# Queries from unnormalised rows, with the norm's factor applied later

## The reference, cut to what matters

```python
x = x + mixed @ w_out[l]
x = x + peer(rmsnorm(x, norm2_g[l]), peer_w_query[l], peer_sub_keys[l], peer_u[l], peer_v[l])
...
q = (xt @ w_query).reshape(T, PEER_HEADS, 2, PEER_DK // 2)
s = jnp.einsum('thpd,phkd->thpk', q, sub_keys)
s_top, i_top = lax.top_k(s, PEER_TOPK)
cand = s_top[:, :, 0, :, None] + s_top[:, :, 1, None, :]
best, pos = lax.top_k(cand, PEER_TOPK)
g = jax.nn.softmax(best, axis=-1)
a = gelu(einsum('thkd,td->thk', u_tab[idx], xt))
out = einsum('thk,thkd->td', g * a, v_tab[idx])
```

## Time and profile before

| what | value |
|---|---|
| median of 3 runs | 1877.42 us (1875.99 to 1878.51) |
| profiled execution | 1873.26 us, span 1871.5 us |
| granted TensorE clock, mean | 0.998 |
| TensorE busy | 1843.8 us, 99% |
| VectorE busy | 1381.0 us, 74% |
| ScalarE busy | 1170.2 us, 63% |
| GpSimd busy | 754.7 us, 40% |

### The profile page before, as it was taken

One profiled execution on the slowest core, in us unless ns is written; L12 is line 12 of the kernel. 1 busy time (PEld: TensorE's weight loads), 2 busy tenths in 40 slices (PEclk: granted clock), 3 DMA queues, 4 the chain that ended last, 5 costly groups with the idle time before them and its releaser, 6 DMA issues.

```text
span 1871.5 us, 38820 instructions
## 1 busy us (share of the span) xinstructions
PE 1843.8 (99%) x11090; PEld 1591.0 (85%) x11090; DVE 1381.0 (74%) x3018; ACT 1170.2 (63%) x2296; POOL 754.7 (40%) x586
## 2 busy tenths in 40 slices
PE   7999999999999999999999999999999999999998
PEld 6889888888888888778888998888888888888886
DVE  6864998888887666776647559987888966666666
ACT  5754666777776555555566446667777765555554
POOL 6551998677770000010063439967777500000000
PEclk9999999999999999999999999999999999999999
DMA  6345555444445575555542545554444455555554
GB/s 217 101 134 160 180 191 191 158 154 146 148 146 180 191 243 206 185 180 186 193 143 76 169 155 188 185 188 162 146 148 145 150 187 196 195 191 191 193 195 150
DMA packets 90500, 320.04 MB, mean 171 GB/s; under 512 B 10304, under 2 KB 11072, under 8 KB 90176
## 3 DMA queue, kind: packets, MB, share of 16 engines
q1 hardware_dynamic: 90432, 319.20, 49.9%
HBM read 318.11 MB, written 1.05 MB: 171 GB/s over the span
## 4 chain that ended last, share of the span: by engine, by line
PE 93%; DVE 3%; ACT 1%; issue 1%; POOL 1%; DMA 0%; SPq 0%; POOLq 0%; DVEq 0%; ACTq 0%
PE ps L919 26%; PE ps L921 13%; PE ps L994 12%; PE ps L996 12%; PE ps L997 12%; PE ps L941 5%; PE ps L892 2%; PE ps L890 2%; PE ps L895 2%; ACT work L1146 1%; PE ps L906 1%; PE ps L605 0%; PE ps L800 0%; PE ps L744 0%; POOL tab_lo L1431 0%
## 5 line engine op out<-in xcount | busy, mean ns | idle before, releaser
L919 PE MATMUL ps<-x_hl,tab_hi 128*128 128x512 f32 x2048 | 725.9, 399 | 0.0
L1492 POOL TENSOR_TENSOR tab_lo<-raw,tab_hi 128x512 fp32r<-128x512 f32 x448 | 575.2, 1298 | 254.6 <-ACT tab_hi L1272 167.0
L921 PE MATMUL ps<-x_hl,tab_lo 128*128 128x256 f32 x2048 | 571.4, 279 | 0.0
L2071 DVE TENSOR_TENSOR tab_lo<-raw,tab_hi 128x512 fp32r<-128x512 f32 x512 | 356.1, 697 | 256.2 <-ACT tab_hi L1384 254.7
L919 PEld LDWEIGHTS ps<-x_hl,tab_hi 128*128 128x128 f32 x2048 | 384.4, 188 | 89.8 <-DVE tab_lo L1965 0.3
L1272 ACT ACTIVATE tab_hi<-raw 128x512 fp32r<-128x512 f32 x504 | 316.0, 630 | 196.5 <-PE ps L921 195.5
L994 PE MATMUL ps<-tab_lo,w_hi 128*128 128x512 f32 x1024 | 399.4, 390 | 0.7 <-DVE w_lo L2111 0.7
L996 PE MATMUL ps<-tab_hi,w_hi 128*128 128x512 f32 x1024 | 398.5, 389 | 0.0
L997 PE MATMUL ps<-tab_hi,w_lo 128*128 128x512 f32 x1024 | 398.4, 389 | 0.0
L921 PEld LDWEIGHTS ps<-x_hl,tab_lo 128*128 128x128 f32 x2048 | 386.0, 188 | 0.0
L1384 ACT ACTIVATE tab_hi<-raw 128x512 fp32r<-128x512 f32 x512 | 320.2, 625 | 92.9 <-PE ps L997 92.2
(11 more groups left out here) (226 smaller groups left out, 2327.5 us busy)
## 6 DMA issues: line engine op xcount, KB each, us to landing
raw<-tab_u SPq DMA_DIRECT2D x256, 512.0 KB, 3.2
raw<-tab_v SPq DMA_DIRECT2D x256, 512.0 KB, 3.2
raw<-w_proj SPq DMA_DIRECT2D x64, 512.0 KB, 3.6
raw<-w_proj SPq DMA_DIRECT2D x16, 384.0 KB, 3.1
work<-cdft SPq DMA_DIRECT2D x8, 256.0 KB, 5.9
work<-sub_keys SPq DMA_DIRECT2D x2, 1024.0 KB, 4.9
work<-pmat SPq DMA_DIRECT2D x4, 304.0 KB, 5.2
x<-x_in SPq DMA_DIRECT2D x2, 512.0 KB, 3.8
```

The costliest lines, as they stand in the source:

```text
L919: mm(ps[:, s, :], hi, x_hl[:, 4 * h + k, :, :].rearrange("p a t -> p (a t)"), start=(h + k == 0), stop=False, skip_group_check=True)
L921: last = mm(ps[:, s, 0:256], lo, x_hi[:, 4 * h + k, :], start=False, stop=(h + k == 4), skip_group_check=True)
L1492: tt(half(tab_lo, s, h), half(raw, s, h), half(tab_hi, s, h).bitcast(F32), ALU.subtract).then_inc(lo_pool.sem, 1)
L2071: v.tensor_tensor(half(tab_lo, s, h), half(raw, s, h), half(tab_hi, s, h).bitcast(F32), ALU.subtract).then_inc(lo_dve.sem, 1)
```

## The change

The rows of x are transposed as they are, without the scaling. Their row pieces (times the gain) go into `x_hi` and `x_lo` and the queries are made from them. TensorE drops the 14 filler matmuls; it transposes channels 0 to 511 (`transpose_rows(0)`, 8 transposes) ahead of query tile 0 and channels 512 to 1023 (`transpose_rows(4)`) behind it. The row pieces are laid so that pieces 0 to 3 fill banks 4 and 5, pieces 4 to 7 banks 6 and 7.

The factor of a token, still the inverse root from GpSimd, is used twice. The exponential of the softmax takes it as its scale, one instruction per block of tokens. For the experts, VectorE multiplies the identity by the factor (`scale_diagonal`), TensorE multiplies ones by that diagonal ahead of query tile 6, which puts the factor of each token in every partition, and ScalarE copies it to SBUF. From the end of query tile 8 on, GpSimd adds the two parts of row piece k and multiplies by the factor (`scale_rows(k)`) as soon as query tile 8+k has used it; ScalarE and VectorE split the result again (`scaled_upper`, `scaled_lower`). TensorE waits for the eighth piece ahead of the experts.

```diff
@@ TensorE
+                def transpose_rows(k0):
+
+                    for b in range(TB):
+                        pe.wait_ge(*at(out_added, l, 12 if k0 else 10 + b))
+                        for k in range(k0, k0 + 4):
+                            last = tr(row_tile(k)[:, b * P:(b + 1) * P], x[:, b, k * P:(k + 1) * P], ident)
+                    last.then_inc(xT_ready.sem, 2)
...
-                keep_clock(14, 1)
-                transpose_x(2, 4)
+                transpose_rows(0)
                 keep_clock(3, 1)
 
                 for n in range(16):
                     part, k = n // 8, n % 8
+                    if n == 1:
+                        transpose_rows(4)
+                    if n == 6:
+                        pe.wait_ge(*at(h_lo, l, 2 * DT))
+                        pe.wait_ge(*at(diag_ready, l, TB))
+                        for b in range(TB):
+                            last = mm(ps[:, 7, b * P:(b + 1) * P], ones, diag[:, b, :], start=True, stop=True)
+                        last.then_inc(scale_ready.sem, 1)
+                    if n == 8:
+                        pe.wait_ge(*at(scale_taken, l, 1))
...
+                pe.wait_ge(*at(scaled_lo, l, DT))
                 u_product(0, True, lo_pool, LO_E)
@@ ScalarE
+                def rows_upper(start, end):
+                    for k in range(start, end):
+                        if k % 4 < 2:
+                            act.wait_ge(*at(xT_ready, l, 6 + 2 * (k // 4)))
+                        else:
+                            act.wait_ge(*at(h_lo, l, DT + k - 1))
+                        fn(x_hi[:, k, :], row_tile(k), ACT.Copy, scale=par("g2", k)).then_inc(h_hi.sem, 1)
...
+                block_squares(0)
+                rows_upper(0, 2)
                 upper(Q0 + 1, 0)
                 upper(Q0 + 1, 1)
-                transposed_upper("g2", 8, 4)
+                rows_upper(2, DT)
+                block_squares(1)
                 for n in range(Q0 + 2, Q0 + 10):
+                    if n == Q0 + 8:
+                        act.wait_ge(*at(scale_ready, l, 1))
+                        fn(token_scale, ps[:, 7, 0:256], ACT.Copy).then_inc(scale_taken.sem, 1)
                     upper(n, 0)
                     upper(n, 1)
...
                 for n in range(Q0 + 10, U0 + 1):
                     upper(n, 0)
                     upper(n, 1)
+                    if n > Q0 + 10:
+                        scaled_upper(n - Q0 - 11)
...
-                fn(best.rearrange("p b h n -> p (b h n)"), best.rearrange("p b h n -> p (b h n)"),
-                   ACT.Exp).then_inc(gate_exp.sem, 1)
+                for b in range(TB):
+                    last = fn(best[:, b, :, :], best[:, b, :, :], ACT.Exp, scale=rinv[:, b:b + 1])
+                last.then_inc(gate_exp.sem, 1)
@@ GpSimd
+                def scale_rows(k):
+
+                    pool.wait_ge(*at(half_used, l, 2 * (Q0 + 8 + k) + 2))
+                    if k >= 2:
+                        pool.wait_ge(*at(scaled_lo, l, k - 1))
+                    tt(scaled[k % 2], x_hi[:, k, :].bitcast(F32), x_lo[:, k, :].bitcast(F32), ALU.add)\
+                        .then_inc(row_sum.sem, 1)
+                    pool.wait_ge(*at(row_sum, l, k + 1))
+                    tt(scaled[k % 2], scaled[k % 2], token_scale, ALU.mult).then_inc(row_scaled.sem, 1)
...
+                pool.wait_ge(*at(scale_taken, l, 1))
+                for k in range(DT - 2):
+                    scale_rows(k)
+                u_lower_half(0, 0, 0)
+                scale_rows(DT - 2)
+                u_lower_half(0, 0, 1)
+                scale_rows(DT - 1)
+                u_lower(0, 1)
@@ VectorE
-                add_group(2, 1, HYENA_BANKS, (1,), (0,))
-                block_mean(0)
-                add_group(2, 1, HYENA_BANKS, (1,), (1,))
-                block_scale(0)
-                block_mean(1)
-                block_scale(1)
-                transposed_lower("g2", 8, 4, 0, 2)
+                add_group(2, 1, HYENA_BANKS, (1,))
+                rows_lower(0, 2)
                 lower(Q0 + 1, 0)
                 lower(Q0 + 1, 1)
-                transposed_lower("g2", 8, 4, 2, DT)
-
+                rows_lower(2, DT)
                 for n in range(Q0 + 2, U0):
                     lower(n, 0)
                     lower(n, 1)
+                    if n == Q0 + 3:
+                        block_mean(0)
+                        block_mean(1)
+                    if n == Q0 + 4:
+                        scale_diagonal(0)
+                        scale_diagonal(1)
+                    if n >= Q0 + 11:
+                        scaled_lower(n - Q0 - 11)
+                scaled_lower(DT - 3)
...
+                scaled_lower(DT - 2)
+                scaled_lower(DT - 1)
```

More of the change, by code:

```diff
@@ L146, in hybrid_encoder, with row_tile @@
         columns = [onehot[:, s, 8 * P:10 * P].bitcast(BF16).rearrange("p (t c) -> p t c", t=4) for s in range(2)]
+        diag = dist_abs[:, 0:TB, :]
+        def row_tile(k):
+            col = (k // 2 % 2) * 256
+            return ps[:, 4 + k % 2 + 2 * (k // 4), col:col + 256]
+        token_scale = sums[:, 0, 0, :]
+        scaled = [sums[:, 1, n, :] for n in range(2)]
         picksf = picks[:, :, :].rearrange("p n t -> p (n t)")
@@ L287, in hybrid_encoder @@
         inv_root = sig("inv_root", 6)
-        xn_done = sig("xn_done", 2 * TB)
+        xn_done = sig("xn_done", TB)
         xT_ready = sig("xT_ready", 8)
@@ L291, in hybrid_encoder @@
         h_lo = sig("h_lo", 16)
+        diag_ready = sig("diag_ready", TB)
+        scale_ready = sig("scale_ready", 1)
+        scale_taken = sig("scale_taken", 1)
+        row_sum = sig("row_sum", DT)
+        row_scaled = sig("row_scaled", DT)
+        scaled_hi = sig("scaled_hi", DT)
+        scaled_lo = sig("scaled_lo", DT)
         fn_m_ready = sig("fn_m_ready", 1)
@@ L1055, in transposed_upper, with scaled_upper @@
                            scale=par(gain, k)).then_inc(h_hi.sem, 1)
+                def rows_upper(start, end):
[5 more added lines that the diff above has]
+                        fn(x_hi[:, k, :], row_tile(k), ACT.Copy, scale=par("g2", k)).then_inc(h_hi.sem, 1)
+                def scaled_upper(k):
+                    act.wait_ge(*at(row_scaled, l, k + 1))
+                    fn(x_hi[:, k, :], scaled[k % 2], ACT.Copy).then_inc(scaled_hi.sem, 1)
                 def spectrum_part(n, bank):
@@ L1241, in _, with block_squares @@
                 upper(Q0, 1)
[L1242 to L1246, removed]
+                def block_squares(b):
+                    for n in range(2 * b, 2 * b + 2):
+                        act.wait_ge(*at(out_added, l, 8 + n + 1))
+                        col = slice((n % 2) * 512, (n % 2 + 1) * 512)
+                        fn(xn[:, n // 2, col], x[:, n // 2, col], ACT.Square, scale=D ** -0.5,
+                           accum_out=ss4[:, n:n + 1]).then_inc(sq_sum.sem, 1)
+                block_squares(0)
+                rows_upper(0, 2)
                 upper(Q0 + 1, 0)
                 upper(Q0 + 1, 1)
-                transposed_upper("g2", 8, 4)
+                rows_upper(2, DT)
+                block_squares(1)
                 for n in range(Q0 + 2, Q0 + 10):
+                    if n == Q0 + 8:
+                        act.wait_ge(*at(scale_ready, l, 1))
+                        fn(token_scale, ps[:, 7, 0:256], ACT.Copy).then_inc(scale_taken.sem, 1)
                     upper(n, 0)
@@ L1258, in _ @@
                     upper(n, 1)
+                    if n > Q0 + 10:
+                        scaled_upper(n - Q0 - 11)
                 upper(U0 + 1, 0)
+                scaled_upper(DT - 2)
                 upper(U0 + 1, 1)
+                scaled_upper(DT - 1)
                 for g in range(4):
@@ L1485, in _, with u_lower_half, u_lower @@
                     inverse_root(5 + b, rinv[:, b:b + 1], ms[:, b:b + 1], 1)
-                def u_lower(i):
-                    for s in range(4):
+                def u_lower_half(i, s, h):
+                    pool.wait_ge(*at(half_used, l, i * 8 + 2 * (U0 + s) + h - 3))
+                    pool.wait_ge(*at(hi_done, l, i * 8 + 2 * (U0 + s) + h + 1))
+                    tt(half(tab_lo, s, h), half(raw, s, h), half(tab_hi, s, h).bitcast(F32),
+                       ALU.subtract).then_inc(lo_pool.sem, 1)
+                def u_lower(i, first=0):
+                    for s in range(first, 4):
                         for h in range(2):
[L1490 to L1493, removed]
+                            u_lower_half(i, s, h)
                 def set_ones(start, end):
@@ L1498, in set_ones @@
                     return nc.gpsimd.memset(area(start + P, end - start - P), 1.0)
+                def scale_rows(k):
[6 more added lines that the diff above has]
+                    tt(scaled[k % 2], scaled[k % 2], token_scale, ALU.mult).then_inc(row_scaled.sem, 1)
                 pool.wait_ge(*at(xT_ready, l, 8))
                 set_ones(UNIT_A, CAND).then_inc(unit_set.sem, 1)
```

(20 more changed lines are left out.)

## The result

The changed kernel takes **1884.35 us** (median of 7 runs, 1882.63 to 1885.58), the kernel before 1877.42 (7 runs): ratio 1.0036, 95% interval 1.0025 to 1.0048. That is slower by 6.9 us, beyond the range of 1874.0 to 1881.2 and beyond the 0.2%. The prediction was wrong. The profiled execution took 1884.05 us, its span is 1882.3 us, its mean granted clock 0.997 (before: 1873.26, 1871.5, 0.998).

A forecast was written before the change was run, and what follows sets the result against it. TensorE, busy 99% of the span, was taken as the bound. Filler removed and the new tile 2 wait nearly cancelled, +0.15 us per layer with the restart: 1877.42 + 0.3 = 1877.7 us, range 1874.0 to 1881.2.

The forecast's parts named there:

- the 0.2%: Whole kernel: about 0.2% (3.75 us) is what a measurement can tell from no change; slower by more had chance 0.12.
- The new start of the queries: Handover from output projection to queries: first query matmul at 126.8 instead of 130.26, tile 0 ending 3.2 us earlier.
- What is late next: Query tile 2: ScalarE's fixed order delays its upper part, so TensorE waits a new 1.95 us, starting at 135.7.
- The rest of the queries: Query tiles 2 to 15 and the ones matmuls: stage ends at 176.5; per layer +0.15 us with the restart.
- Costed at nothing: Side work on VectorE, ScalarE, GpSimd and SyncE, including diagonals, filling of ones and exponential: no time added.
- The clock: Rival: new idle stretches lower TensorE's clock, one fall per layer costing 3.4 us in all, 1881.1 us; chance 0.12.
- GpSimd too slow for the experts' rows: Rival, ahead of the experts: above 1.4 us an operation GpSimd ends late; at 1.73 us, 1888.3 us; chance 0.05.
- far from any wait of TensorE: Softmax exponential on ScalarE: becoming two instructions was said to delay no wait of TensorE and cost nothing.
- the sum: Whole kernel: the earlier median of 1877.42 us plus 0.3 us for two layers gives 1877.7 us.

The follow-up runs named there:

- three kernels: Changed kernel with, in turn: diagonals from two SBUF inputs (1878.42 us), GpSimd's filling of ones later (1877.71 us), that filling cut into eight (1877.98 us).
- the first experiment: Changed kernel, but VectorE makes the diagonals by multiplying two SBUF tensors instead of by a scalar: 1878.42 us, ratio 1.0015 to the kernel before.
- the other run: Changed kernel with 8 filler matmuls of the identity put in front of query tile 5: 1881.8 us, ratio 1.0035 to the kernel before.
- its second profile: Changed kernel run a second time with nothing altered: 1882.09 us, ratio 1.0034 to the kernel before.

## Why the prediction was wrong

- **The new start of the queries: right.** First query matmul at 126.84 (126.8), third at 127.36 (127.35), second transposes at 130.09 (129.95).
- **What is late next: right, and by the cause named.** Row pieces 4 to 7, then the squares, then the upper part of tile 2:

```profile
131.16 0.84 ACT L1096 ACTIVATE x_hl<-ps,pv 128x256 fp32r<-128x256 f32 x2 [2.24 <-PE ps L613]
132.19 0.87 ACT L1096 ACTIVATE x_hl<-ps,pv 128x256 fp32r<-128x256 f32 x2 [0.19 <-DVE x_hl L1935]
...
134.18 2.18 ACT L1073 ACTIVATE tab_hi<-raw 128x512 fp32r<-128x512 f32 x4
```

  This is ScalarE in the changed kernel, at 131.16, 132.19 and 134.18 where I had 131.15, 132.17 and 134.2. Moving the squares took 1.2 of the 1.74 us away.
- **The rest of the queries: right in itself.** Without the second wait the stage is 52.14 to 52.16 us in three kernels, forecast 52.21 (52.06 + 0.15).
- **"Costed at nothing": this step failed.** It says "The diagonal needs the root about 137 and VectorE reaches it by 140; tile 6 is due at 147" and, two sentences on, "GpSimd's filling of ones moves some 8 us later and still ends near 146". VectorE reached the diagonal at 140.22 and the filling ended at 145.67, both within 0.4 us of that (the root came at 138.6, 1.6 us later than said, to no effect). I costed each edit against its own consumer (tile 6, the first scaling at 156) and never laid one beside the other. Side by side they are a scalar-form instruction of VectorE and a GpSimd instruction of 6.6 us, and VectorE stood still until that one ended. And the loss isn't at the diagonal's consumer: it is at tile 5, whose subtraction is queued behind it on VectorE. That subtraction starts at 145.74 here and at 141.06 in the first experiment, 4.7 us apart; VectorE was ahead of TensorE by most of that, and 1.96 us were left.
- **The rule that says so was cited, for another pair.** "SBUF — State Buffer", section "SBUF: two separate sides", of the Trainium skill says which pairs of VectorE and GpSimd instructions exclude one another, and for how long: a VectorE instruction in one of its two-port modes waits for a whole GpSimd instruction of any kind, one with two SBUF inputs only for a GpSimd instruction that reads SBUF. The runs agree: one input 5.4 us, two inputs 0.28 us beside a filling that reads nothing, and less when the GpSimd instruction is cut; held over three pieces, as in layer 1 there, is more than the rule says. That the diagonal runs in a two-port mode is an inference, since either form of it takes 0.28 us alone; on a larger instruction the one-input form is the quicker, 1024 elements in 0.75 us against 0.69 for 512 of two inputs. I had applied it to the scalings of the experts' rows, where it changed little, and not to the filling.
- **The clock: right rival, wrong argument.** I gave it 0.12 on the ground that 1.98 us idle had left the clock at 1.00. It fell once per layer at the 1.7 us said, behind 1.96 us here and behind 1.75 us in the other run. One row of no fall is no bound, and the later profiles show it at the very place of that row: behind a wait of 1.98 to 2.00 us there the clock fell in four of ten. In the kernel with the squares moved and the diagonals in the other form:

```profile
958.83 0.41 PE L645 MATMUL ps<-tab_lo,x_hl 128*128 128x384 f32 x1 [1.98 <-POOL tab_lo L1490]
```

```profile
955.00:959.00 4.00, 2.02 (x12) 1.73 (x11) 2.87 (x8) 1.61 (x4) 3.71 (x2) 1.00 0.13 54
958.00:964.00 6.00, 5.17 (x21) 5.20 (x22) 0.00 (x0) 1.25 (x3) 5.55 (x6) 0.72 0.43 122
```

  The first of these stretches is that of rows 8, and it reads 1.00 here too: it ends too soon behind the wait to tell. In the kernel before, the clock stays at 1.00 from 958 to 964 as well, so what I said of it was true, but the row shown didn't prove it. And the fall adds to any new wait of this length, as it did to mine. Its price belonged to the forecast itself, by a share of executions.
- **GpSimd too slow for the experts' rows: did not happen.** Single groups of the changed kernel, as in the page's part 5 (busy, mean ns):

```profile
L1566 POOL TENSOR_TENSOR sums<-x_hl 128x256 f32<-128x256 f32 x16 | 12.0, 749 | 38.9 <-PE ps L927 38.9
...
L1569 POOL TENSOR_TENSOR sums<-sums 128x256 f32<-128x256 f32 x16 | 16.2, 1013 | 1.3
```

  0.75 and 1.01 us a piece, against 0.72 estimated and a limit of 1.4. From the scores' start to the first expert tile it is 7.1 us, as before.
- **The exponential "far from any wait of TensorE": a small miss.** ScalarE's two exponentials take 0.69 us where one took 0.42; GpSimd's wait for the upper part behind them is 2.23 us where it was 1.96, and TensorE's weight load waits for GpSimd's subtraction in turn:

```profile
287.47 0.19 PEld L951 LDWEIGHTS ps<-x_hl,tab_hi 128*128 128x128 f32 x1 [0.40 <-POOL tab_lo L1548]
```

  That is 0.2 to 0.3 us per layer, not tested by a run of its own.
- **What the sum hasn't got even so.** With the second wait and its fall gone, three kernels are still 1.0013 to 1.0015 of the kernel before, 2.4 to 2.8 us, where I had 0.3. The stage gives 0.2 us of it and the exponentials about 0.5; part of the rest is in the expert phase, and its cause is open.

## What to carry to other kernels

When an edit moves a long GpSimd instruction, list every VectorE instruction that will now lie beside it, and its form: one of scalar form with one input can stand still to the end of it, and holds all that is queued behind. A form with two inputs, or the long instruction cut in pieces, costs nothing to write; of the two the form is the surer, since the pair of diagonals beside the cut filling still took 2.46 us in one layer. And a new idle stretch of TensorE of near 2 us is priced with the clock's fall (here 1.7 us) in a share of executions; where it comes from one in-order queue, first ask what may stand behind the late piece instead of ahead of it.

## What was not expected of the hardware

- **The same short wait drops the clock in one execution and not in the next.** 1.74 us at tile 2 left it at 1.00 in the changed kernel's profile, 1.75 us dropped it to 0.72 over 6 us in the kernel with filler at tile 5. Of twelve waits of 1.74 or 1.75 us there two dropped it; of eleven waits of 1.98 to 2.00 us, one in each profile where layer 1's work begins, four did. What decides it is open.
- **A pace of the experts' matmuls that is not explained.** The expert phase with table u is 144.4 us long in both layers of the kernel before and of its version without filler; in the changed kernel it is 145.5 in both (144.7 in both in its second profile), in four others 145.5 in one layer or both and 144.6 to 144.7 in all the rest. In the long ones a pair of matmuls takes 0.355 us instead of 0.347 from about 100 us into the phase on, with no wait recorded, at a clock of 1.00. Layers of one execution differ. Of the 18 layers profiled with some form of the change 8 go at the slow pace, of the 4 without it none, and it begins where the exponentials stand (ScalarE 284.83, 97.5 us into the phase); that hints at the change as its cause, but 4 layers are few. This is some 1 us per layer of the 10.8 us between the two profiled spans, and part of why medians of versions with equal query stages lie 0.1% apart. No run here isolates it.
